# A gated recurrence's decay levels between 128-token blocks, replaced by 128x128 states carried from block to block

## What is computed

```python
"""S_t = diag(f_t) S_{t-1} + k_t v_t^T ; o_t = S_t^T q_t"""
o_fwd = gla_chunk_scan(qh, k_f, ih, lf_f)
flip = lambda t: jnp.flip(t, axis=2)
o_bwd = flip(gla_chunk_scan(flip(qh), flip(k_b), flip(ih), flip(lf_b)))
```

## Time and profile before

| | |
|---|---|
| median of 3 runs | 1439.61 us (1438.82 to 1440.43) |
| the profiled execution | 1438.98 us |
| its span, first to last instruction | 1437.2 us |
| PE busy | 1404.3 us, 98% |
| DVE, ACT, POOL busy | 59%, 43%, 50% |
| mean granted clock of PE | 0.996 |

### The profile page before, as it was taken

One profiled execution on the slowest core, in us unless ns is written; L12 is line 12 of the kernel. 1 busy time (PEld: TensorE's weight loads), 2 busy tenths in 40 slices (PEclk: granted clock), 3 DMA queues, 4 the chain that ended last, 5 costly groups with the idle time before them and its releaser, 6 DMA issues.

```text
span 1437.2 us, 18656 instructions
## 1 busy us (share of the span) xinstructions
PE 1404.3 (98%) x6444; PEld 1119.2 (78%) x6444; DVE 842.7 (59%) x1051; ACT 623.3 (43%) x894; POOL 724.7 (50%) x551
## 2 busy tenths in 40 slices
PE   5999999999999999999999999999999999999999
PEld 4887777777788888888878877776777888888887
DVE  6666598555677667700267857973557677675001
ACT  6343455475444444422343335554744444443211
POOL 2597275426444444444577853752473444444443
PEclk9999999999999999999999999999999999999999
DMA  4212112113222222323222221121122223222323
GB/s 151 89 61 91 54 60 73 49 43 101 75 101 102 88 92 98 102 91 102 90 86 74 89 77 46 55 74 44 60 90 86 90 99 102 88 95 95 103 94 110
DMA packets 36820, 121.05 MB, mean 84 GB/s; under 512 B 4896, under 2 KB 5408, under 8 KB 36768
## 3 DMA queue, kind: packets, MB, share of 16 engines
q1 hardware_dynamic: 36480, 119.64, 24.9%
q10 hardware_dynamic: 288, 0.72, 0.1%
HBM read 114.05 MB, written 2.10 MB: 81 GB/s over the span
## 4 chain that ended last, share of the span: by engine, by line
PE 81%; POOL 5%; issue 5%; ACT 4%; DVE 4%; DMA 1%; SPq 0%; POOLq 0%; DVEq 0%; ACTq 0%
PE bank L494 23%; PE bank L496 22%; PE bank L495 22%; PE bank L578 3%; POOL wL L434 2%; PE bank L599 2%; PE bank L546 2%; PE bank L617 2%; PE bank L534 2%; POOL wL L428 1%; POOL rstd L358 1%; PE bank L587 1%; DVE QQ L1229 1%; PE bank L608 1%; ACT wH L758 1%
## 5 line engine op out<-in xcount | busy, mean ns | idle before, releaser
L434 POOL TENSOR_TENSOR wL<-raw,wH 128x1024 fp32r<-128x1024 f32 x142 | 342.3, 2411 | 420.4 <-ACT wH L766 357.9
L494 PE MATMUL bank<-hH,wH 128*128 128x512 f32 x1216 | 487.9, 401 | 25.2 <-POOL wL L428 12.1
L496 PE MATMUL bank<-hL,wH 128*128 128x512 f32 x1216 | 476.2, 392 | 0.0
L495 PE MATMUL bank<-hH,wL 128*128 128x512 f32 x1216 | 475.7, 391 | 0.0
L428 POOL TENSOR_TENSOR wL<-raw,wH 128x256 fp32r<-128x256 f32 x272 | 255.1, 967 | 188.7 <-ACT wH L758 188.7
L494 PEld LDWEIGHTS bank<-hH,wH 128*128 128x128 f32 x1216 | 229.5, 189 | 96.5 <-issue 39.4
L496 PEld LDWEIGHTS bank<-hL,wH 128*128 128x128 f32 x1216 | 229.5, 189 | 49.7
L495 PEld LDWEIGHTS bank<-hH,wL 128*128 128x128 f32 x1216 | 229.9, 189 | 44.8 <-issue 0.5
L766 ACT ACTIVATE wH<-raw 128x1024 fp32r<-128x1024 f32 x116 | 122.5, 1056 | 183.6 <-PE bank L496 180.9
L758 ACT ACTIVATE wH<-raw 128x1024 fp32r<-128x1024 f32 x95 | 100.4, 1057 | 150.7 <-PE bank L496 150.1
L494 PE MATMUL bank<-gH,wH 128*128 (+1 forms) x352 | 137.3, 390 | 0.1
(11 more groups left out here) (156 smaller groups left out, 1718.2 us busy)
## 6 DMA issues: line engine op xcount, KB each, us to landing
raw<-wts SPq DMA_DIRECT2D x211, 512.0 KB, 3.3
x<-xT SPq DMA_DIRECT2D x8, 256.0 KB, 5.4
swp<-K SPq DMA_DIRECT2D x32, 64.0 KB, 2.0
swp<-QO SPq DMA_DIRECT2D x32, 64.0 KB, 2.3
outT<-x SPq DMA_DIRECT2D x8, 256.0 KB, 2.0
raw<-wts ACTq DMA_DIRECT2D x1, 512.0 KB, 4.2
W<-pos SPq DMA_DIRECT2D x1, 256.0 KB, 7.4
R<-par SPq DMA_DIRECT2D x2, 109.0 KB, 3.6
```

The costliest lines, as they stand in the source:

```text
L434: pool.tensor_tensor(wL[:, s, :], raw[:, s, :], wH[:, s, :].bitcast(F32), ALU.subtract)\
L494: pe.matmul(out, wH[:, s, a:a + P], rhs_h, start=first, stop=False)
L495: pe.matmul(out, wL[:, s, a:a + P], rhs_h, start=False, stop=False)
L496: return pe.matmul(out, wH[:, s, a:a + P], rhs_l, start=False, stop=last)
```

## The change

Levels 8, 9 and 10 and all blocks of `A` off the diagonal are gone. After level 7, queries and keys are already decayed to the edges of their 128-token block. So for each head and direction the keys of three blocks are transposed (`to_keys`, items 8 and 9, copied to `KTOK` by the scalar engine), multiplied with the values to one 128x128 matrix for each block (`carry`, the forward direction in item 10, the backward one at the end of that slot), and added up from block to block, with the block's total decay, to the states `ST` (`states`, vector engine). `gather` then adds, for each block of 128 tokens, the block on the diagonal and the two products of queries with states, in the middle of the slot of item 11. `hi` 0 and 1 are projected earlier (units 10 and 11), `hq` 2 and 3 later (15 and 16). `A` is cut to its diagonal blocks; with `KTOK` and `ST` it takes the same room. The diff, without the renumbered semaphore counts:

```diff
-         ("zf", 2), ("zf", 3), ("zb", 2), ("zb", 3), ("hq", 2), ("hq", 3),
-         ("dk", 0), ("dq", 0), ("dv", 0), ("hi", 0), ("hi", 1),
+         ("zf", 2), ("zf", 3), ("zb", 2), ("zb", 3), ("hi", 0), ("hi", 1),
+         ("dk", 0), ("dq", 0), ("dv", 0), ("hq", 2), ("hq", 3),
...
-LEVELS = 11
-ITEMS = 2 * (LEVELS + 1)
+LEVELS = 8
+TURN_F, TURN_B, CARRY, OUT = 8, 9, 10, 11
+PAIR_ITEMS = 12
+ITEMS = 2 * PAIR_ITEMS
...
-        A = sb("A", [P, 2, TT, S], F32, mix)
+        A = sb("A", [P, 2, TT, P], F32, mix)
+        KTOK = sb("KTOK", [P, 2, 2, TT - 1, P], F32, mix)
+        ST = sb("ST", [P, 2, 2, TT - 1, P], F32, mix)
...
+        def carried(d):
+
+            return list(range(TT - 1)) if d == 0 else list(range(TT - 1, 0, -1))
...
-                        if n is not None and 1 <= n % (LEVELS + 1) <= 8:
-                            grow(*divmod(n, LEVELS + 1))
+                        if n is not None and 1 <= n % PAIR_ITEMS < LEVELS:
+                            grow(*divmod(n, PAIR_ITEMS))
...
-                        if lv == LEVELS:
-                            pe.wait_ge(*bank6_free.at(l, BANK6[("tokens", ("hi", 2 * pair + 1))] + 1))
-                            for r in range(2):
-                                hd = 2 * pair + r
-                                pe.wait_ge(*a_cp.at(l, 8 * pair + 6 + r + 1))
-                                for i in range(TT):
-                                    m = pe.matmul(bank[2 + r][:], HI[:, i, hd * P:hd * P + P], A[:, r, i, :],
-                                                  start=i == 0, stop=i == TT - 1)
-                                m.then_inc(av_mm.sem, 1)
+                        if lv in (TURN_F, TURN_B):
+                            to_keys(pair, lv - TURN_F)
+                        if lv == CARRY:
+                            carry(pair, 0)
+                        if lv >= LEVELS:
                             return
...
-                                    else:
-                                        m = pe.matmul(o, head(KK, i % 2, hd, i, 1), head(QQ, 1 - i % 2, hd, i ^ 1, 1),
-                                                      start=True, stop=True)
...
-                                half = lv - 9
-                                for i in range(2):
-                                    m = pe.matmul(b[:, i * 2 * P:(i + 1) * 2 * P], head(KK, half, hd, 2 * half + i, 1),
-                                                  head(QQ, 1 - half, hd, 2 - 2 * half, 2), start=True, stop=True)
...
+                    def to_keys(pair, d):
+
+
+                        if d == 0:
+                            pe.wait_ge(*hg_k.at(l, 7 * pair + 7))
+                        for r in range(2):
+                            if d == 0:
+                                pe.wait_ge(*a_msk.at(l, 14 * pair + 12 + r + 1))
                             else:
+                                pe.wait_ge(*kt_ready.at(l, 4 * pair + r + 1))
+                            for n, i in enumerate(carried(d)):
+                                m = pe.transpose(bank[2 + r][:, n * P:n * P + P], head(KK, d, 2 * pair + r, i, 1),
+                                                 cst_at(C_IDENT))
+                            m.then_inc(kt_mm.sem, 1)
+
+                    def carry(pair, d):
+
+                        if d == 0:
+                            pe.wait_ge(*bank6_free.at(l, BANK6[("tokens", ("hi", 2 * pair + 1))] + 1))
+                        for r in range(2):
+                            hd = 2 * pair + r
+                            if d == 0:
+                                pe.wait_ge(*kt_ready.at(l, 4 * pair + 2 + r + 1))
+                            else:
+                                pe.wait_ge(*st_ready.at(l, 4 * pair + r + 1))
+                            for n, i in enumerate(carried(d)):
+                                m = pe.matmul(bank[2 + r][:, n * P:n * P + P], KTOK[:, r, d, n, :], HI[:, i, hd * P:hd * P + P],
+                                              start=True, stop=True)
+                            m.then_inc(kv_mm.sem, 1)
+
+                    def gather(pair):
+
+                        pe.wait_ge(*hg_q.at(l, 9 * pair + 9))
+                        for r in range(2):
+                            hd = 2 * pair + r
+                            pe.wait_ge(*st_ready.at(l, 4 * pair + 2 + r + 1))
+                            for i in range(TT):
+                                o = bank[2 + r][:, i * P:i * P + P]
+                                pe.matmul(o, HI[:, i, hd * P:hd * P + P], A[:, r, i, :], start=True, stop=False)
+                                if i > 0:
+                                    m = pe.matmul(o, ST[:, r, 0, i - 1, :], head(QQ, 1, hd, i, 1), start=False, stop=i == TT - 1)
+                                if i < TT - 1:
+                                    m = pe.matmul(o, ST[:, r, 1, TT - 2 - i, :], head(QQ, 0, hd, i, 1), start=False, stop=True)
+                            m.then_inc(av_mm.sem, 1)
...
                         half(s, 0)
...
+                        n = item_of(s)
+                        if n is not None and n % PAIR_ITEMS == OUT:
+                            gather(n // PAIR_ITEMS)
                         if step_of(s - 1) is not None:
                             turn(step_of(s - 1))
                         half(s, 1)
...
+                        if n is not None and n % PAIR_ITEMS == CARRY:
+                            carry(n // PAIR_ITEMS, 1)
                         if step_of(s - 1) is not None:
                             values(step_of(s - 1))
...
+                        if lv in (TURN_F, TURN_B):
+                            d = lv - TURN_F
+                            for r in range(2):
+                                act.wait_ge(*kt_mm.at(l, 4 * pair + 2 * d + r + 1))
+                                if pair:
+                                    act.wait_ge(*kv_mm.at(l, 2 * d + r + 1))
+                                act.activation(KTOK[:, r, d, :, :].rearrange("p n c -> p (n c)"), bank[2 + r][:, 0:3 * P], ACT.Copy)\
+                                   .then_inc(kt_ready.sem, 1)
...
+                        if item_of(s) is not None and item_of(s) % PAIR_ITEMS == OUT:
+                            recurrent_out(item_of(s) // PAIR_ITEMS)
...
-                        if 1 <= lv <= 8:
+                        if 1 <= lv < LEVELS:
...
+                    def states(pair, d):
+
+
+
+                        if d == 0:
+                            dve.wait_ge(*tot_ready.at(l, 7 * pair + 7))
+                        f = totals(pair, P)
+                        for r in range(2):
+                            dve.wait_ge(*kv_mm.at(l, 4 * pair + 2 * d + r + 1))
+                            if pair:
+                                dve.wait_ge(*av_mm.at(l, r + 1))
+                            for n, i in enumerate(carried(d)):
+                                kv = bank[2 + r][:, n * P:n * P + P]
+                                if n == 0:
+                                    ch(dve.tensor_copy(ST[:, r, d, n, :], kv))
+                                    continue
+                                new = dve.scalar_tensor_tensor(ST[:, r, d, n, :], ST[:, r, d, n - 1, :], f[:, d, i:i + 1], kv,
+                                                               ALU.mult, ALU.add)
+                                if n == 1:
+                                    ch(new)
+                            new.then_inc(st_ready.sem, 1)
...
+                        n = item_of(s)
+                        if n is not None and n % PAIR_ITEMS == OUT:
+                            states(n // PAIR_ITEMS, 1)
                         if step_of(s - 1) is not None:
                             combine(step_of(s - 1))
...
+                            if lv == CARRY:
+                                states(pair, 0)
                         if step_of(s) is not None:
                             row_max(step_of(s))
```

More of the change, by code:

```diff
@@ L589, in item @@
-                            m.then_inc(lv_mm.sem, 1)
+                            for i in range(TT):
+                                o = b[:, i * P:i * P + P]
+                                if lv == 0:
+                                    m = pe.matmul(o, kx[:, r, i * P:i * P + P], head(QQ, 1, hd, i, 1),
+                                                  start=True, stop=True)
+                                else:
+                                    h = 2 ** (lv - 1)
+                                    m = pe.matmul(o.rearrange("p (n two h) -> p n two h", two=2, h=h),
+                                                  kx[:, r, i * P:i * P + P], crossing(QQ, hd, i, h, 0),
+                                                  start=True, stop=True)
@@ L831, in item @@
                     def item(n):
-                        pair, lv = divmod(n, LEVELS + 1)
-                        for r in range(2):
-                            if lv == LEVELS:
```

(33 more changed lines are left out.)

77 lines of the change are left out of this document (36 added, 41 removed).

## The result

The changed kernel takes 1429.46 us, the median of 4 runs (1427.0 to 1430.04), beside 1439.47 us for the kernel before (4 runs, 1438.82 to 1440.43): a ratio of 0.9928, 95% interval 0.9916 to 0.9940. Repeated on another occasion with five runs it was 0.9937 (0.9924 to 0.9951), so 9 to 10 us are gained. The forecast was 1427.8 us (1424.3 to 1433.0). The profiled execution after took 1427.0 us, with a span of 1425.2.

The account below looks back on a forecast made before the run. The matmul engine's instructions, one after another, were taken as the bound in the edited slots. Terms -2.78, -1.57 and twice -3.75 gave -11.85 us, so 1427.1 for the profiled execution, plus 0.6 for the median: 1427.8 us (1424.3 to 1433).

Parts of the forecast that it names:

- Paces: Matmul engine time from one group's start to the next: 0.107 to 0.111 us per 128-column fp32 record, 0.435 per 512-column record.
- Pair 0, layer 0: Slots 11 to 18 of layer 0, first pair of heads: slot changes on the matmul engine summing to -2.78 us.
- the late `kx`: Layer 0, slot 12: scalar engine copies tokens before its table loads, so `kx` ends at 105.8, delaying slot 13 by 0.1 us.
- slot 15 at nothing: Slot 15: the smaller item saves 1.1 us, which returns as wait for `ev`, evicted only after the previous slot's `rope`: 0.
- Pair 0, layer 1: Same slots in layer 1: -1.57 us, with slot 11 at +1.73 instead of +0.42 because the vector engine evicts late behind `forget`.
- Pair 1: Slots 27 to 30, both layers, no tokens moved: -1.07, -1.0, +0.9 and -2.58, summing to -3.75 us per layer.
- Beside it: Other engines and DMA: `states` about 2 us on the vector engine, 1.5 to 3 us left before `gather`; no added time.
- Rival B: Slots 18 and 30: `states` lasts 7.4 us, `gather` waits about 2 us at four places, 1435.8 us; chance 0.10.
- A: Everything is hidden: `ev` isn't late in slot 15 (-1.1 us per layer) nor slot 11 (-1.3), 1424.3 us; chance 0.08.
- C: Slot 15: the matmul engine's clock falls around the wait between transposes, up to +6 us, 1434; chance 0.04.
- D: New small matmuls are bound by weight loads, 0.19 us per record, giving about 1449 us; chance 0.03.
- E: Waits in slots 31 to 34, where the scalar engine's `Silu` is late, take the gain back: 1437 to 1441; chance 0.02.

Follow-up runs that it names:

- order A: The changed kernel with `hq` 2 as unit 10, `hi` 0 as 11, `hi` 1 as 15, so nothing is transposed in slot 11: 1428.25 us, ratio 0.9929 to the kernel before.
- the cut item: The kernel before with item 11 (`HI` times `A`) cut into 128-column matmuls, 64 records for 16: 1438.91 us; the item 7.24 us against 6.96.
- order B: The changed kernel with `hq` 2, `hi` 0, `hq` 3, `hi` 1, `dv` 0 as units 10, 11, 14, 15, 16: 1425.23 us, ratio 0.9906 to the kernel before.

## Why the prediction was right

**Paces.** Right, and the change hangs on them: 0.112 us per 128-column record in `gather` (0.107 to 0.111 forecast), 1.43 for a `carry` (1.28, and 1.38 with seam), transposes 0.57 for six ahead of a unit (0.64).

**Pair 0, layer 0: -2.26 instead of -2.78.** By slot, from one start to the next:

| slots | forecast | measured | from |
|---|---|---|---|
| 11, 12 | +0.94 | +1.16 | 14.50 to 15.66 us |
| 13, 14 | 0 | +0.09 | 16.21 to 16.30 |
| 15 | 0 | 0.00 | 8.49 to 8.49 |
| 16 | -1.58 | -1.65 | 7.77 to 6.12 |
| 17 | +0.44 | +0.65 | 8.84 to 9.49 |
| 18 | -2.58 | -2.50 | 15.83 to 13.33 |

In 11 and 12 the late `kx` costs more than the 0.1 I gave it. The forecast's 105.8 stands on the scale of before, where slot 12 starts at 98.11; here it starts at 97.98. Counted from there, `kx` ended after 7.85 us and not 7.72, mostly because the copy of the tokens took 0.6 us and not 0.5. The matmul engine would have been ready for slot 13 after 7.71 us (7.66 forecast) and started it after 7.95: 0.24 of wait. In 17 a seam of 0.15 also stands behind the second `carry`. The step that mattered, slot 15 at nothing, is exact: its row shows 1.69 us of wait where 1.7 was forecast.

**Pair 0, layer 1: -1.30 instead of -1.57.** Slot 11's +1.73 came out to the hundredth, with `ev` as the cause: in order A the wait went with the move, and the kernel before with the new order lost 1.27 there. What is off is again the size of the other terms: slots 16 to 18 give -3.50 and not -3.72.

**Pair 1: -3.71 instead of -3.75**, in both layers.

**Beside it.** `states` takes 1.96 us, 2 forecast; in slots 18 and 30 of layer 0 `gather` starts 2.4 and 3.3 us after it has ended (147.8 to 150.24, 278.5 to 281.84). Rival B falls by the price of 0.29 and 0.35 us per operation. (The 0.865 us that the forecast took as the 512-column price without GpSimd is a mean of six at 0.745 and two at 1.22, and the two ran beside GpSimd: a grouped row can hide two prices.) B was wrong in place too: tripled, `states` is felt first by `row_max` and `scores`, not by `gather`. I had named `row_max` and costed it at nothing for 1 to 3 us; that held, and the run shows it would not have held for 6.

**Rivals.** A: `ev` is late at both places. C: the granted clock is 1.00 in slot 15 in all the profiled executions. D: refuted by the cut item and by `gather` itself (its 0.215 us for a record of 256 columns should read 0.225, 1.80 / 8, which changes nothing). E: nothing is taken back behind slot 31 by the scalar engine, where the wait on `rstd` is 0.67 us before and after; but one part of it is there by another way, the +1.2 us of layer 0's feed-forward loop, whose passes take 22.17 us instead of 22.07. It is in every version after, and in none before. The tripled `states` and the 48 instructions show that such a loop can move by some 5 us with what the vector engine does ahead of it; that the 0.1 of a pass comes from there too isn't shown, since 16 more instructions left it as it was. Its cause stays open.

**Sum.** -11.85 forecast, -10.98 in the edited stretches. With +1.2 from the loop it is -9.8, and the medians differ by 10.0. The forecast of 1427.8 us was 1.7 below the median. Its parts were off by 2.1: 0.8 us too much gain in pair 0, 0.1 in pair 1, and 1.2 of loss unseen. So the total agreed a little better than its parts deserved, by an amount that the runs vary by anyway. Two of the signs named beforehand agreed by luck. Slot 19 of layer 0 started 2.83 us earlier and slot 31 6.54 (2.8 and 6.5 forecast), but 0.57 of both lies ahead of slot 7, where nothing was edited; from slot 7 on it is 2.26 and 5.97.

## What to carry to other kernels

When an item on the bounding engine is made shorter, look at what it covered: here a shorter item ahead of a late `ev` gave nothing back in slot 15, and a move of units that took `to_tokens` out from behind `rope` and `forget` (order B) was worth another 2.8 us in the edited stretches. On this engine in fp32, matmuls of 128 columns cost in proportion to their columns (0.112 against 0.435 us per record), so sparse or blocked forms can be priced by columns. And compare the unedited stretches too: with `states` done three times, a loop far behind it cost 4.7 us more. Padding isn't free either: 48 instructions that only step a semaphore made the vector engine's next instruction some 4.5 us late.

## What the hardware showed unexpectedly

**A half-clock stretch behind a 1.9 us wait, sometimes.** At the first unit of each layer's up-projection loop the matmul engine waits 1.9 us on `wL`. In 8 of the 26 such places in the 13 profiled executions the granted clock then fell to half, in the kernel before, layer 1, from 1097.2 to 1100.6 us:

```profile
1097.04 0.64 PE L494 MATMUL bank<-hH,wH 128*128 128x512 f32 x1 [1.94 <-POOL wL L434]
1097.48 0.63 PE L495 MATMUL bank<-hH,wL 128*128 128x512 f32 x1
1097.90 0.63 PE L496 MATMUL bank<-hL,wH 128*128 128x512 f32 x1
```

Matmuls start 0.43 us apart here instead of 0.227, and a stretch costs 1.7 us. It explains a good part of the difference between executions of one kernel: after had none (1427.0 us, the lowest of its runs), the same kernel again had one (1429.6). Of these 2.6 us, 1.6 lie there and 1.2 ahead of slot 7, where every execution has a wait of 7 us and a half-clock stretch that reaches beyond it: in the one, matmuls start again at 34.97 and run at half clock up to 38.72, in the other from 35.58 to 40.47. The wait of 1.7 us in slot 15 with transposes on both sides never led to one.

**Holds of 2 us in a loop on the vector engine**, which move with what the engine does ahead of the loop, as above: 2.40 us for a copy of 0.17, and some 5 us on the kernel's time. Why an instruction is held isn't shown.
